# Loading the query weights ahead of the third modulation chunk, and projecting the queries in two contraction halves

## The chip, the cores and the metric

The kernel runs on one core of one Trainium2 chip. The metric is device time in microseconds (us), the median of repeated executions. The core has a tensor engine for matrix products (PE; its weight loads are listed as PEld), a vector engine (DVE), a scalar engine (ACT), GpSimd (POOL), and a sync engine (SP) whose in-order instruction stream issues nearly all of the large transfers.

## The reference, cut to what matters

Two transformer blocks are computed on 256 tokens of width 1024, in float32. Only the opening of the first block bears on the change:

```
sh1, sc1, gt1, sh2, sc2, gt2 = modulation(c, w_mod, b_mod)      # silu(c) @ w_mod + b_mod, 6 x 1024 columns
hx = rms_norm(x, norm1_g) * (1 + sc1) + sh1                     # 256 tokens
hc = rms_norm(ctx, norm1_g) * (1 + csc1) + csh1                 # 256 context rows, same w_mod with c_ctx
q, k, v, gb, gc, u = split(hx @ w_in)                           # 512 | 128 | 128 | 512 | 512 | 512 columns
q, k = rms_norm per head of 64, then rotary for the tokens of x
```

From the context only k and v are used. Then come attention, a short convolution of `gc * u` gated by `gb`, the output projection, a mixture of 32 experts (each with three weight matrices of 3 MB), and a second block with retention, stick-breaking attention and a SwiGLU layer.

## The kernel before

**Layout.** `hT` holds the normalized inputs turned, as 8 contraction blocks (c = 0 to 7) of 128 rows by 512 columns: columns 0 to 255 are the context (row tiles t = 0, 1), 256 to 511 the tokens (t = 2, 3). `PS` is the accumulator memory, 8 banks of 512 columns. Shift and scale enter `hT` in two halves. Half 0 (blocks 0 to 3) needs the modulation chunks W_A 0 and 1, half 1 (blocks 4 to 7) the chunks W_A 2 and 3. When a half's modulation is turned (`turned_A`), the vector engine forms the scales (lines 1107 to 1115) and modulates the context columns (line 1119), and the scalar engine the token columns (line 723).

**The ring of weights.** The list `order` (line 297) gives the order in which SP issues the weight chunks of this opening, and the slot of each. All are 2 MB except the key and value weights W_KV (1 MB). Before an issue, SP waits until the chunk that held the same slot has been used (line 492): W_GB goes into the slot of W_A 2, W_B 2 into that of W_A 3, W_GC into that of W_B 0, W_U into that of W_B 1, W_B 3 into that of W_Q. W_Q has the wait of line 500 besides, on the second normalized tile.

**The tensor engine's order** (lines 2012 to 2040). `keys_values(0)` multiplies the first four blocks for all four row tiles into banks 4 to 7 and leaves the sums open. `modulate_A(2)`, `modulate_A(3)` and `turned_A(1)` follow, with `keep_busy` matmuls of no use to the result between them. `keys_values(1)` closes the sums. `project` computes the queries of t = 2 and then of t = 3, 8 blocks each. `conv_blocks(W_GB, 0)` follows, then the transposes of the finished queries and keys (line 2030, behind `qk_ready` 4), then `conv_blocks(W_GC, CV)`, the first attention scores, and the rest of the modulation (`modulate_B`).

**The vector engine's order** (lines 1134 to 1170). In this order it treats the keys of t = 0 and t = 1 (norm only), `accumulated(0)` and `accumulated(1)`, the queries and keys of t = 2 (sums of squares, gains, norm and rotary, lines 1143 to 1166), `accumulated(2)`, the queries and keys of t = 3, and `accumulated(3)`. An `accumulated(k)` multiplies the 128 by 4096 chunk W_B k by a column of the condition and adds it to the sum so far, so that the tensor engine can do the first four of the eight W_B chunks in one pass (lines 1127 and 1130). The end of `accumulated(1)` frees the slot for W_GC, that of `accumulated(2)` the slot for W_U. The scalar engine copies the projections out of `PS` and squares them (lines 737 to 745), and GpSimd forms the reciprocal roots (lines 622 to 624).

Of the kernel before, what the change touches and what calls it, by code (L numbers as in the profile page):

```python
# [10 lines left out]
ACT = mybir.ActivationFunctionType  # L11
AX = mybir.AxisListType.X

P = 128
D = 1024
KD = D // P
# [53 lines left out]
def build(nc, A, out):  # L70

    ctx = ExitStack()
    with ctx:
# [4 lines left out]
        PS = ctx.enter_context(nc.psum_tensor("PS", [P, 8, 512], F32))  # L78
# [20 lines left out]
        def shaped(ap, *dims):  # L99
            if len(dims) == 2:  # L100
                return ap.rearrange("p (a b) -> p a b", a=dims[0])
            if len(dims) == 3:
                return ap.rearrange("p (a b c) -> p a b c", a=dims[0], b=dims[1])
            return ap

        def flat(ap):
            return ap.rearrange("p a b -> p (a b)")
# [70 lines left out]
        hT = slot4.take(KD, 512)  # L178
# [91 lines left out]
        S = {}  # L270
        for n in ("ld_consts ld_x ld_ctx ld_c ld_vec ld_rows cleared set_cond cond_ready "
# [22 lines left out]

        W_A, W_B, W_KV, W_Q, W_GB, W_GC, W_U = range(7)
        ACC = 3
        order = [(W_A, 0, 0), (W_A, 1, 1), (W_KV, 0, 4), (W_A, 2, 2), (W_A, 3, 3), (W_Q, 0, 5), (W_B, 0, 0), (W_B, 1, 1),
                 (W_GB, 0, 2), (W_B, 2, 3), (W_GC, 0, 0), (W_U, 0, 1), (W_B, 3, 5), (W_B, 4, 3), (W_B, 5, 2), (W_B, 6, 0), (W_B, 7, 5)]
        columns = {W_KV: (512, 256), W_Q: (0, 512), W_GB: (768, 512), W_GC: (1280, 512), W_U: (1792, 512)}
        freed = {W_Q: ("qkv_psum", 6), W_GB: ("gbgc_psum", 4), W_GC: ("gbgc_psum", 8), W_U: ("u_psum", 4)}  # L300
# [14 lines left out]
        def chunk(kind, i=0):  # L315
            if kind == W_KV:
                return w_kv
            home = ring[slot_of[kind, i]]
            if kind == W_A:
                return shaped(home, KD, CW)  # L320
            return home if kind == W_B else shaped(home, KD, CW)

        def chunk_landed(eng, kind, i=0):
            eng.wait_ge(w_full[slot_of[kind, i]], landed[kind, i])
# [97 lines left out]
        def chunk2(name, i):  # L422
            n = C2[name, i]
            dims = seconds[n][1]
            size = 1
            for d in dims:
                size *= d
            return shaped(cslots[:, n % CSLOTS, 0:size], *dims)
# [54 lines left out]
        def _(sp):  # L483
# [100 lines left out]
            for n, (src, dims, _, _) in enumerate(seconds):  # L584
                if n >= CSLOTS:
                    sp.wait_ge(S[seconds[n - CSLOTS][2]], seconds[n - CSLOTS][3])
                size = 1
                for d in dims:
                    size *= d
                dst = shaped(cslots[:, n % CSLOTS, 0:size], *dims)  # L590
                parts = [(dst[:, :, u], src[:, :, u]) for u in range(2)] if len(dims) == 3 else [(dst, src)]
                for to, of in parts:
                    sp.dma_start(to, of).then_inc(c_full[n % CSLOTS], 16)
# [85 lines left out]
        def _(a):  # L679
# [47 lines left out]
            def head_sumsq(t):  # L727

                if t >= 1:
                    a.wait_ge(S["qksq_sum"], t)  # L730
                a.drain()
                o = 512 if t < 2 else 0
                a.activation(qk_sq[:, o:640], qk[:, t, o:640], ACT.Square).then_inc(S["qksq_done"], 1)
# [7 lines left out]
            for t in range(2, 4):  # L741
                a.wait_ge(S["qkv_psum"], t + 3)
                a.activation(qk[:, t, 0:512].rearrange("p (j g d) -> p g j d", g=2, j=4),
                             PS[:, t, :].rearrange("p (g j d) -> p g j d", g=2, j=4), ACT.Copy).then_inc(S["qkv_evac"], 1)
                head_sumsq(t)

            for m in range(8):
# [1137 lines left out]
        def _(pe):  # L1885
            mm = pe.matmul
# [7 lines left out]
            def keep_busy(bank, n):  # L1894

                for _ in range(n):
                    mm(PS[:, bank, 0:P], ident, ident, start=True, stop=True, skip_group_check=True)
# [15 lines left out]
            def modulate_A(k):  # L1913

                half, u, w = k // 2, k % 2, chunk(W_A, k)
                chunk_landed(pe, W_A, k)
                for c in range(KD):
                    for gg in range(4):
                        last = mm(PS[32 * gg:32 * gg + 32, 1 - half, P * u:P * u + P], condT[:, c, :], w[:, c, P * gg:P * gg + P],
                                  start=c == 0, stop=c == KD - 1, skip_group_check=True)  # L1920
                last.then_inc(S["mod_psum"], 1)

            def turned_A(half):

                pe.wait_ge(S["modA_evac"], half + 1)
                transposes(2 + half, [modA[:, P * n:P * n + P] for n in (2 * half, 2 * half + 1)]).then_inc(S["modT_psum"], 1)
# [35 lines left out]
            for c in range(KD):  # L1962
                last = pe.transpose(PS[:, 3, META * c:META * c + META], metahn[:, P * c:P * c + P], ident[0:META, 0:META])
# [1 line left out]
            turned_A(0)  # L1965


            def project(bank, kind, t):

                w = chunk(kind)  # L1970
                width = columns[kind][1]
                for c in range(KD):
                    last = mm(PS[:, bank, 0:width], hT[:, c, P * t:P * t + P], w[:, c, :], start=c == 0, stop=c == KD - 1)
                last.then_inc(S["qkv_psum"], 1)

            def keys_values(half):

                w = chunk(W_KV)
                for t in range(4):
                    for c in range(4 * half, 4 * half + 4):  # L1980
                        if t in (0, 2):
                            pe.wait_ge(S["hTc_ready" if t == 0 else "hTx_ready"], c + 1)
                        last = mm(PS[:, 4 + t, 0:256], hT[:, c, P * t:P * t + P], w[:, c, :], start=c == 0, stop=c == KD - 1,
                                  skip_group_check=True)
                    if half:
                        last.then_inc(S["qkv_psum"], 1)
# [26 lines left out]
            chunk_landed(pe, W_KV)  # L2013
            pe.wait_ge(S["xnT_evac"], 8)
            keys_values(0)
            modulate_A(2)
            keep_busy(1, 2)
            modulate_A(3)
            keep_busy(1, 1)
            turned_A(1)  # L2020
            keep_busy(1, 4)
            keys_values(1)
            chunk_landed(pe, W_Q)
            for t in range(2, 4):
                project(t, W_Q, t)
            pe.wait_ge(S["qkv_evac"], 4)
            conv_blocks(W_GB, 0)
            pe.wait_ge(S["qk_ready"], 4)
# [13 lines left out]
            for b in range(2):  # L2042
                last = mm(PS[:, 6 + b, :], K["headmean"], flat(sqT)[:, 512 * b:512 * b + 512], start=True, stop=True)
# [83 lines left out]
            for i in range(KD // 2):  # L2127
                for k in range(2):
                    mm(PS[64 * k:64 * k + 64, 6, TOK:TOK + 1], w_route[:, 2 * i + k, :], shT[:, 2 * i + k:2 * i + k + 1],
                       start=i == 0, stop=i == KD // 2 - 1, skip_group_check=True)  # L2130
# [9 lines left out]
            for t in range(TT + 1):  # L2140
                rows = lgT[:, P * t:P * t + P] if t < TT else lgT[:, TOK:TOK + 1].to_broadcast([P, P])
                last = mm(PS[:, 7, NR * t:NR * t + EG + E], rows, K["fold"], start=True, stop=True, skip_group_check=True)
# [95 lines left out]
            for n in range(4):  # L2238
                t, h = n // 2, n % 2
# [5 lines left out]
            def block_T(bank, w, col, rhs, n, off=0, start=True, halves=False):  # L2245

                for c in range(KD):
                    if halves and c == KD // 2:
                        pe.wait_ge(S["hnT_ready"], 2)
                    last = mm(PS[:, bank, off:off + n], w[:, c, col:col + P], rhs(c), start=c == 0, stop=c == KD - 1,  # L2250
                              skip_group_check=True)
                return last
# [160 lines left out]
            for n in range(2 * RH):  # L2413
                name, h = ("rq" if n < RH else "rk"), n % RH
                chunk2_landed(pe, name, h // 2)
                w = chunk2(name, h // 2)
# [7 lines left out]
                for i in range(2):  # L2424
                    last = block_T(2 * (n % 2) + i, w, 256 * (h % 2) + P * i, x_of if n < RH else all_of,
                                   TOK if n < RH else LK)
# [4 lines left out]
            for h in range(RH):  # L2431
# [3 lines left out]
                for keys, q0, off in ((META, 0, 0), (META + P, P, TOK)):  # L2435
                    for d in range(2):
                        mm(PS[:, 4 + h % 2, off:off + TOK - q0], kR[:, 2 * h + d, keys:keys + P], qR[:, 2 * h + d, q0:TOK],
                           start=d == 0, stop=d == 1, skip_group_check=True)
                for d in range(2):
                    for gg in range(4):  # L2440
                        last = mm(PS[32 * gg:32 * gg + 32, 6 + h % 2, 0:TOK], kR[:, 2 * h + d, 0:32], qR[:, 2 * h + d, :],
                                  start=d == 0, stop=d == 1, skip_group_check=True)
# [32 lines left out]
            for h in range(RH):  # L2475
# [6 lines left out]
                for cc in range(2):  # L2482
                    for gg in range(4):
                        last = mm(PS[32 * gg:32 * gg + 32, 3, :], hnT[:, 2 * gg + cc, 0:32], rv[:, 2 * gg + cc, :],  # L2484
                                  start=cc == 0, stop=cc == 1, skip_group_check=True)
# [104 lines left out]
            w = chunk2("fi", 0)  # L2590
            for t in range(TT):
                pe.wait_ge(S["hnT_ready"], 3 + t)
                for u in range(2):
                    for i in range(2):
                        for c in range(KD):
                            o = TOK * i + P * t
                            last = mm(PS[:, u, o:o + P], w[:, c, u, P * i:P * i + P], hnT[:, c, P * t:P * t + P],  # L2597
                                      start=c == 0, stop=c == KD - 1, skip_group_check=True)
# [60 lines left out]
            def out_product(j, k):  # L2659

                bank, x, w = out_products(j)[k]
                return mm(PS[:, bank, :], x, w, start=j == 0, stop=j == FB // 2 - 1, skip_group_check=True)  # L2662

            for j in range(2 * FO_MAIN):
                if j % 2 == 0:
                    pe.wait_ge(S["combined"], fo_combined("w", j // 2))
                for k in range(7):
# [6 lines left out]
                    last = out_product(j, k)  # L2674
# [4 lines left out]
            for k in range(7):  # L2679
                for j in range(2 * FO_MAIN, FB // 2):  # L2680
                    if k == 0 and j % 2 == 0:
                        pe.wait_ge(S["combined"], fo_combined("w", j // 2))
                    last = out_product(j, k)
# [70 lines left out]
```

## Time and profile before

| what | value |
|---|---|
| median of 3 runs | 1547.5 us (1546.63 to 1547.79) |
| the profiled execution | 1550.47 us |
| its span in the trace | 1548.7 us |
| mean granted clock of the tensor engine | 0.936 of 2.4 GHz |
| PE, DVE, ACT, POOL busy | 83%, 35%, 13%, 2% of the span |

The profiled execution is 1.8 us longer than its span and 3.0 us longer than the median. The opening up to the first attention scores takes the first 96 us of the span. The experts run from 196 us to about 861 us and move most of the bytes.

### The profile page before, as it was taken

How to read it: one execution, taken by the hardware profiler on the slowest of the kernel's cores; microseconds unless marked ns; L12 is line 12 of the kernel's file. 1: busy time of each engine (PE TensorE's matmuls, PEld its weight loads, DVE VectorE, ACT ScalarE, POOL GpSimd, SP SyncE). 2: the span in 40 equal slices, each digit the busy share in tenths (PEclk: the TensorE clock that was granted, in tenths of full speed). 3: DMA queues.
4: the chain of work that ended last, by engine and by line, in shares of the span. 5: the costliest groups of instructions: out<-in, count | busy, mean ns of one | idle time of the engine just before them, and what ended most of it. 6: DMA issues, size and time to landing. Idle time of an engine off the chain costs nothing.

```text
span 1548.7 us, 25300 instructions
## 1 busy us (share of the span) xinstructions
PE 1284.8 (83%) x11090; PEld 834.0 (54%) x11090; DVE 542.5 (35%) x977; ACT 204.1 (13%) x429; POOL 33.8 (2%) x66
## 2 busy tenths in 40 slices
PE   6999977666666666666665999999999999999998
PEld 5786555344333333333433766458544477688843
DVE  1556432111111111111111312752446463466654
ACT  4214200000000000000000223320011211211101
POOL 1101000000000000000000100000000000000000
PEclk9999999888888888888877999999999999999999
DMA  9879999999999999999999733333244344445551
GB/s 348 317 304 324 381 390 428 431 430 432 430 431 431 430 433 428 431 431 430 432 428 422 265 120 109 140 132 140 103 156 145 109 155 171 134 145 174 173 190 54
DMA packets 86431, 447.43 MB, mean 289 GB/s; under 512 B 4012, under 2 KB 27728, under 8 KB 72672
## 3 DMA queue, kind: packets, MB, share of 16 engines
q1 hardware_dynamic: 84096, 441.20, 71.1%
q10 hardware_dynamic: 1008, 3.77, 0.6%
q0 software_dynamic: 1264, 1.55, 0.4%
q8 instruction: 48, 0.79, 0.2%
q14 instruction: 15, 0.12, 0.0%
HBM read 445.44 MB, written 1.06 MB: 288 GB/s over the span
## 4 chain that ended last, share of the span: by engine, by line
PE 55%; DMA 33%; issue 5%; DVE 3%; DVEq 1%; ACT 1%; POOL 1%; POOLq 0%; ACTq 0%
DMA mem<-in_w_down 33%; PE PS L2613 8%; PE PS L2250 8%; PE PS L2268 7%; PE PS L2456 6%; PE PS L2206 5%; PE PS L2662 4%; PE PS L2189 2%; PE PS L2075 2%; PE PS L1999 2%; PE PS L1891 2%; PE PS L1901 2%; PE PS L2567 1%; PE PS L2597 1%; PE PS L2484 0%
## 5 line engine op out<-in xcount | busy, mean ns | idle before, releaser
L2189 PE MATMUL PS<-mem 128*32 128x192 f32 x4096 | 207.2, 362 | 106.3 <-DMA mem<-in_w_up 72.4
L2189 PEld LDWEIGHTS PS<-mem 128*32 128x32 f32 x4096 | 150.4, 122 | 157.1 <-DMA mem<-in_w_up 82.1
L2206 PE MATMUL PS<-mem 128*32 128x256 f32 x1536 | 137.3, 530 | 99.4 <-DMA mem<-in_w_down 91.9
L2206 PEld LDWEIGHTS PS<-mem 128*32 128x32 f32 x1536 | 62.3, 148 | 167.4 <-DMA mem<-in_w_down 98.0
L2268 PE MATMUL PS<-mem 128*128 128x256 f32 (+1 forms) x392 | 125.1, 474 | 2.6 <-issue 1.1
L2613 PE MATMUL PS<-mem 128*128 128x256 f32 x560 | 122.6, 379 | 0.0
L2250 PE MATMUL PS<-mem 128*128 128x256 f32 (+1 forms) x512 | 117.2, 390 | 0.0
L1365 DVE TENSOR_TENSOR mem<-mem,PS 128x192 f32<-128x192 f32 x32 | 11.3, 354 | 298.7 <-ACT mem L803 298.7
L2613 PEld LDWEIGHTS PS<-mem 128*128 128x128 f32 x560 | 105.6, 190 | 14.2 <-ACT mem L1037 0.3
L2250 PEld LDWEIGHTS PS<-mem 128*128 128x128 f32 x512 | 97.4, 192 | 18.6 <-issue 1.8
L2456 PE MATMUL PS<-mem 128*128 128x512 f32 x224 | 98.4, 594 | 0.7 <-ACT mem L938 0.7
L2268 PEld LDWEIGHTS PS<-mem 128*128 128x128 f32 x392 | 72.9, 190 | 46.4 <-issue 38.8
L1369 DVE TENSOR_TENSOR mem<-PS,mem 128x256 f32<-128x256 f32 x32 | 13.6, 425 | 196.4 <-PE PS L2206 196.4
L2456 PEld LDWEIGHTS PS<-mem 128*128 128x128 f32 x224 | 41.9, 190 | 53.3 <-issue 51.8
L2662 PE MATMUL PS<-mem 128*128 128x512 f32 x154 | 66.4, 592 | 0.0
L801 ACT ACTIVATE mem<-PS 128x256 f32<-128x256 f32 x32 | 12.3, 384 | 338.3 <-PE PS L2167 338.3
L2213 PE MATMUL PS<-mem 32*128 32x256 f32 x512 | 36.7, 400 | 17.6 <-DVE mem L1369 17.6
L803 ACT ACTIVATE mem<-PS 128x192 f32<-128x192 f32 x32 | 10.6, 331 | 302.8 <-PE PS L2189 302.8
L1901 PEld LDWEIGHTS PS<-mem 128*128 128x128 f32 x296 | 35.4, 145 | 26.6 <-issue 11.6
L1901 PE MATMUL PS<-mem 128*128 128x128 f32 x296 | 42.8, 283 | 7.2 <-DVE mem L1445 2.4
L2662 PEld LDWEIGHTS PS<-mem 128*128 128x128 f32 x154 | 29.2, 190 | 35.9 <-issue 35.9
L2213 PEld LDWEIGHTS PS<-mem 32*128 32x128 f32 x512 | 23.1, 184 | 37.1 <-DVE mem L1369 36.4
(340 smaller groups left out, 1341.2 us busy)
## 6 DMA issues: line engine op xcount, KB each, us to landing
mem<-in_w_gate SPq DMA_DIRECT2D x31, 3072.0 KB, 38.7
mem<-in_w_down SPq DMA_DIRECT2D x31, 3072.0 KB, 38.7
mem<-in_w_up SPq DMA_DIRECT2D x30, 3072.0 KB, 39.4
mem<-in_w_in SPq DMA_DIRECT2D x26, 2048.0 KB, 7.8
mem<-in_w_mod SPq DMA_DIRECT2D x12, 2048.0 KB, 17.6
mem<-in_w_ffn_in SPq DMA_DIRECT2D x22, 1024.0 KB, 6.7
mem<-in_w_ffn_out SPq DMA_DIRECT2D x5, 2048.0 KB, 7.9
mem<-in_w_ret_out SPq DMA_DIRECT2D x4, 2048.0 KB, 7.9
```

Source lines behind the costliest of these rows:

```text
L1891: last = mm(PS[0:m, bank, 0:n], lhs(c), w[:, c, col0:col0 + n], start=c == 0, stop=c == KD - 1)
L1901: last = pe.transpose(PS[:, bank, rows * i:rows * i + rows], s, ident[0:rows, 0:rows])
L1999: last = mm(PS[:, 6 + m % 2, 0:TOK], w[:, c, P * (m % 4):P * (m % 4) + P], hT[:, c, TOK:2 * TOK], start=c == 0, stop=c == KD - 1)
L2075: last = mm(PS[:, 2 + n, :], mixT[:, first + c, P * t:P * t + P], weights[:, c, CW * o:CW * o + CW], start=start and c == 0, stop=stop and ...
L2189: last = mm(PS[32 * gg:32 * gg + 32, 2 * h + 1, 192 * j:192 * j + 192], xTe[:, h, c, :], rows[:, 192 * gg:192 * gg + 192], start=c == 0 an ...
L2206: last = mm(PS[32 * gg:32 * gg + 32, 2 * h, 0:256], hTe[:, h, j, :], slots[:, 3 * h + 2, o:o + 256], start=j == 0, stop=j == JE - 1, skip_ ...
L2213: last = mm(PS[:, 4 + gg, 256 * t:256 * t + 256], back[own, h, P * t:P * t + P], yexp[own, h, :], start=False, stop=True, skip_group_check ...
L2250: last = mm(PS[:, bank, off:off + n], w[:, c, col:col + P], rhs(c), start=c == 0, stop=c == KD - 1, skip_group_check=True)
L2268: last = mm(PS[:, bank, 0:width], x[:, c, :], w[:, c, :], start=product in ("m1", "m2", "m7") and c == 0, stop=product in ("m2", "m4", "m3 ...
L2456: last = mm(PS[:, bank, :], x[:, c, :], w[:, c, :], start=start and c == 0, stop=stop and c == 3, skip_group_check=True)
L2613: last = mm(PS[:, fi_bank(bank, j), 0:256], x[:, c, :], part[:, c, :], start=start and c == 0, stop=stop and c == 3, skip_group_check=True)
L2662: return mm(PS[:, bank, :], x, w, start=j == 0, stop=j == FB // 2 - 1, skip_group_check=True)
```

## The change

The query weights are issued before W_A 2 and 3 and not behind them. `project`, which ran behind `keys_values(1)`, gives way to `queries(half)`: `queries(0)` multiplies blocks 0 to 3 for t = 2 and t = 3 straight after `keys_values(0)` and leaves both sums open, and `queries(1)` closes them behind `keys_values(1)`. The queries accumulate in banks 1 and 2, and no longer in 2 and 3, since `turned_A(1)` writes bank 3 in between. The `keep_busy` matmuls around `modulate_A(3)` are left out, and the last ones go to bank 0.

```
-        order = [(W_A, 0, 0), (W_A, 1, 1), (W_KV, 0, 4), (W_A, 2, 2), (W_A, 3, 3), (W_Q, 0, 5), (W_B, 0, 0), (W_B, 1, 1),
+        order = [(W_A, 0, 0), (W_A, 1, 1), (W_KV, 0, 4), (W_Q, 0, 5), (W_A, 2, 2), (W_A, 3, 3), (W_B, 0, 0), (W_B, 1, 1),
@@ scalar engine, evacuation of the queries
-                             PS[:, t, :].rearrange("p (g j d) -> p g j d", g=2, j=4), ACT.Copy).then_inc(S["qkv_evac"], 1)
+                             PS[:, t - 1, :].rearrange("p (g j d) -> p g j d", g=2, j=4), ACT.Copy).then_inc(S["qkv_evac"], 1)
@@ tensor engine
-            def project(bank, kind, t):
-
-                w = chunk(kind)
-                width = columns[kind][1]
-                for c in range(KD):
-                    last = mm(PS[:, bank, 0:width], hT[:, c, P * t:P * t + P], w[:, c, :], start=c == 0, stop=c == KD - 1)
-                last.then_inc(S["qkv_psum"], 1)
+            def queries(half):
+
+                w = chunk(W_Q)
+                for t in (2, 3):
+                    for c in range(4 * half, 4 * half + 4):
+                        last = mm(PS[:, t - 1, :], hT[:, c, P * t:P * t + P], w[:, c, :], start=c == 0, stop=c == KD - 1,
+                                  skip_group_check=True)
+                    if half:
+                        last.then_inc(S["qkv_psum"], 1)
@@
             keys_values(0)
+            chunk_landed(pe, W_Q)
+            queries(0)
             modulate_A(2)
-            keep_busy(1, 2)
             modulate_A(3)
-            keep_busy(1, 1)
             turned_A(1)
-            keep_busy(1, 4)
+            keep_busy(0, 4)
             keys_values(1)
-            chunk_landed(pe, W_Q)
-            for t in range(2, 4):
-                project(t, W_Q, t)
+            queries(1)
             pe.wait_ge(S["qkv_evac"], 4)
             conv_blocks(W_GB, 0)
```

## Rows read from the trace of the kernel before

**Rows 1.** The page: span, and the chain that ended last, by line.
```profile
span 1548.7 us, 25300 instructions
DMA mem<-in_w_down 33%; PE PS L2613 8%; PE PS L2250 8%; PE PS L2268 7%; PE PS L2456 6%; PE PS L2206 5%; PE PS L2662 4%; PE PS L2189 2%; PE PS L2075 2%; PE PS L1999 2%; PE PS L1891 2%; PE PS L1901 2%; PE PS L2567 1%; PE PS L2597 1%; PE PS L2484 0%
```

**Rows 2.** Chain of waits, 0 to 190 us: start, duration, what.
```profile
80.46 0.33 DVE mem L1165
...
81.07 1.53 PE PS L1901 x12
82.61 13.81 PE PS L1999 x64
```

**Rows 3.** Timeline of PE: start, duration, line, operation, count, idle before and releaser.
```profile
31.13 7.14 PE L1983 MATMUL PS<-mem 128*128 128x256 f32 x32 [0.51 <-DVE mem L1119]
38.20 1.95 PE L1919 MATMUL PS<-mem 128*32 128x128 f32 x64
...
40.73 1.95 PE L1919 MATMUL PS<-mem 128*32 128x128 f32 x64
...
43.19 0.44 PE L1901 MATMUL PS<-mem 128*128 128x128 f32 x2
...
44.93 7.17 PE L1983 MATMUL PS<-mem 128*128 128x256 f32 x32 [0.41 <-DVE mem L1119]
51.94 13.90 PE L1973 MATMUL PS<-mem 128*128 128x512 f32 x32
65.68 13.98 PE L1999 MATMUL PS<-mem 128*128 128x256 f32 x64
81.07 1.53 PE L1901 MATMUL PS<-mem 128*128 128x128 f32 x12 [1.42 <-DVE mem L1166]
```

**Rows 4.** Timeline of DVE, 52 to 92 us.
```profile
52.28 2.35 DVE L1127 TENSOR_SCALAR mem<-mem 128x4096 f32<-128x4096 f32 x1
...
60.46 0.82 DVE L1143 TENSOR_REDUCE mem<-mem 128x10 f32<-128x640 f32 x1 [1.27 <-ACT mem L733]
...
68.63 4.48 DVE L1130 SCALAR_TENSOR_TENSOR mem<-mem 128x4096 f32<-128x4096 f32 x1 [0.16 <-issue]
73.03 0.81 DVE L1143 TENSOR_REDUCE mem<-mem 128x10 f32<-128x640 f32 x1
...
80.70 0.32 DVE L1166 TENSOR_TENSOR mem<-mem 128x160 f32<-128x160 f32 x1
87.05 4.49 DVE L1130 SCALAR_TENSOR_TENSOR mem<-mem 128x4096 f32<-128x4096 f32 x1 [6.03 <-DMA mem<-in_w_mod]
```

**Rows 5.** SP's issues of W_A 2, W_Q and W_GB, each with its time to landing.
```profile
L495 SPq DMA_DIRECT2D mem<-in_w_mod x1: 5204/5204/5204, 14.6 to 14.6; - x1
...
DMA to landing us min/median/max: 18.9/18.9/18.9
...
L502 SPq DMA_DIRECT2D mem<-in_w_in x1: 4489/4489/4489, 25.1 to 25.1; - x1
...
DMA to landing us min/median/max: 19.2/19.2/19.2
...
L502 SPq DMA_DIRECT2D mem<-in_w_in x1: 378/378/378, 40.2 to 40.2; - x1
...
DMA to landing us min/median/max: 19.4/19.4/19.4
```

**Rows 6.** Timeline of PE: first matmuls after idle stretches of 1.4 to 4.5 us.
```profile
25.16 3.60 PE L1919 MATMUL PS<-mem 128*32 128x128 f32 x64 [2.04 <-DMA mem<-in_w_mod]
...
244.70 2.80 PE L2206 MATMUL PS<-mem 128*32 128x256 f32 x48 [1.42 <-DVE mem L1367]
...
303.45 5.26 PE L2206 MATMUL PS<-mem 128*32 128x256 f32 x48 [4.50 <-DMA mem<-in_w_down]
```

**Rows 7.** Stages: window, length, busy PE, PEld, DVE, ACT, POOL, granted clock, DMA share, GB/s.
```profile
26.00:27.00 1.00, 1.00 (x28) 0.92 (x21) 0.00 (x0) 0.00 (x0) 0.00 (x0) 0.50 1.04 378
304.00:306.00 2.00, 2.00 (x24) 0.87 (x20) 0.00 (x0) 0.00 (x0) 0.00 (x0) 0.50 0.97 418
```

## The prediction

> **What bounds the kernel now.** I read the page first. Its chain that ended last runs for a third of the span through the expert weights, then through the matmuls of the second block; of the opening only small shares show [rows 1]. The opening feeds what follows without slack: the first expert weights are issued behind semaphores that the tensor engine raises late in the opening (mod_psum 9 and later ones), so a shift of the opening's end shifts the start of the expert stream by as much. What the change is worth must therefore be read from the first 100 us.
>
> There I read the chain of waits. At 81 us it steps from the vector engine's last rotary instruction (line 1166) to the tensor engine's transposes of queries and keys, and stays on the tensor engine from there, first with the 13.8 us of the W_GC block [rows 2]. The tensor engine's timeline says how close that is. It is busy almost without a gap from 31 us, ends the W_GB block at 65.68 + 13.98 = 79.66, and sits idle 1.42 us until line 1166 is done [rows 3]. So two chains end at 81 us: the tensor engine's, with 1.4 us to spare, and the vector engine's, which ends last.
>
> The vector engine's timeline shows what the second is made of: `accumulated(0)` at 52.28, then `accumulated(1)`, then t = 2 from 60.46 to 68.5, `accumulated(2)` from 68.63, t = 3 from 73.03 to 81.02 [rows 4]. In all this it waits for the projections only once, 1.27 us ahead of 60.46, for the square of the queries of t = 2 [rows 4]; waits of about 2 us on GpSimd's roots lie inside each of the two treatments and stay there. So the chain hangs on the time at which it starts, and that is the time at which `keys_values(1)` runs (44.93), since the keys of t = 0 and t = 1 stand first in the vector engine's order.
>
> **The change part by part.** Everything is worked out in the profiled execution.
>
> *Order of the transfers.* The fourth issue (W_A 2 before) landed at 14.6 + 18.9 = 33.5, the sixth (W_Q before) at 25.1 + 19.2 = 44.3 [rows 5]. All of these are 2 MB, so I let the places keep their times: W_Q lands at 33.5, W_A 2 at about 39.0 (the fifth place, in the middle), W_A 3 at 44.3. The wait on the second normalized tile, which now stands in front of two W_A issues on SP, costs nothing: the tile is the second result of the whole vector engine, and SP comes to the wait only behind its issue of W_KV, at 14.6 [rows 5].
>
> *queries(0).* It starts when `keys_values(0)` ends, at 31.13 + 7.14 = 38.2, and W_Q has landed 4.7 us earlier. It is half of the 16 products that took 13.90 us [rows 3], 6.95 us, and ends at 45.15.
>
> *modulate_A(2), (3), turned_A(1).* W_A 2 (39.0) is there. Without the filler between them the two modulations take 1.95 us at most each, where 2.53 us passed from start to start before (38.20 to 40.73) [rows 3]: 0.6 us saved. `modulate_A(3)` wants W_A 3 at about 47.1 and that lands at 44.3, so it waits for nothing, with 2.8 us to spare. The filler left out behind it lay within the wait for the scalar engine's copy and saves nothing. From the start of `modulate_A(3)` to that of `keys_values(1)` it is 44.93 - 40.73 = 4.2 us, a path through the scalar and the vector engine with four filler matmuls over it, unchanged.
>
> So `keys_values(1)` starts 6.95 - 0.6 = 6.35, say 6.3 us later, at 51.2, and with it everything that follows from the second half of the modulation.
>
> *queries(1).* `keys_values(1)` ends at 58.4, and 6.95 us later, at 65.3, the queries are complete (65.8 before). For the tensor engine the change is a gain of 0.5 to 0.6 us. t = 2 is complete at 58.4 + 3.5 = 61.9, and 1.6 us behind that (51.94 + 6.95 = 58.9 to 60.46 before) its squares can be summed: 63.5.
>
> *The vector engine.* `accumulated(0)` starts at 52.28 + 6.3 = 58.6. It and `accumulated(1)` took until 60.46 - 1.27 = 59.2; now until 65.5. The squares of t = 2 have been there since 63.5, so the wait of 1.27 us goes, and nothing else does. t = 2 runs from 65.5, and from there all is as before, 5.0 us later (6.3 - 1.27): `accumulated(2)` at 73.7 (W_B 2, needed at 68.6 before, comes no later than then), t = 3 until 81.0 + 5.0 = 86.1. The tensor engine has ended the W_GB block at 65.3 + 13.98 = 79.3 and waits 6.8 us for it. **The transposes start 5.0 us late.**
>
> *Slots and queues behind it.* W_GB waits for `modulate_A(2)`, now done at 47.1 where its issue was at 40.2. It landed at 40.2 + 19.4 = 59.6, after so long because it stood behind others in the queue [rows 5], which are still there at 47.1. I expect it at about 59.6 again; at worst it takes the full 19.4 us anew and lands at 66.5, 1.2 us after it is wanted, which the 6.8 us of idle time would hide. W_GC is issued at the end of `accumulated(1)`, 6.3 us late, and wanted at 87.6; even if it took the 19.4 us of W_GB it would be there at 84.9. W_U and W_B 3 go with `accumulated(2)`, 5.0 us late, and with them `accumulated(3)`, which waited for W_B 3 until 87.05 [rows 4]. All of this is the same shift of 5.0 and adds nothing.
>
> *The clock.* Not covered by any of this is what 6.8 us of idle time do to the tensor engine. After 2.04 us idle the 64 matmuls of one `modulate_A` took 3.60 us [rows 6] where they take 1.95 [rows 3], and the granted clock was 0.50, the 1.2 GHz level [rows 7]: a loss of 1.65 us. After 4.50 us idle 48 matmuls took 5.26 us where the same took 2.80 after 1.42 us idle [rows 6], a loss of 2.46, again at 0.50 [rows 7]. The stretch of 6.8 us is longer than both. I bound the cost by 0 and 2.5 us and take 1.7, near the first: there the tensor engine had a long unbroken run of work behind the gap, as here. The loss falls on the transposes and on the W_GC block, which stand on the chain [rows 2], and is not made up.
>
> The Trainium skill (TensorE: Matmul & The Clock Gate, "What's actually happening") says of the ramp that for modeling it is under 1% of a typical span and that one should not fit to a count of slow matmuls. By that the term would be left out and the kernel would come to 1552.5. This case's trace shows 1.65 and 2.46 us for single ramps, small against the span, though a third of the effect here.
>
> **The sum.** 5.0 + 1.7 = 6.7 us on the profiled execution of 1550.5. The same shift on the median of 1547.5, which is 3.0 us below it, gives 1554.2.
>
> **The rivals.**
>
> *The clock holds, or its loss is hidden* (12%): 5.0 us alone, 1552.5. For it: the idle time of 1.42 us at 81 us cost nothing. Against it: each of the longer gaps above did.
>
> *The tensor engine sets the end* (8%), the rival on the other side, not slower. Then the 0.6 us of filler counts and the vector engine doesn't: 1546.9, no measurable change. It holds if the vector engine ends t = 3 before 79.3, so if its chain is 7 us shorter than I have it. That wants the two large accumulations (2.35 and about 4.5 us) to be out of the way before the second half of the keys comes. For it speaks that W_B 0 and 1 are issued early, right behind W_A 3. Against it: they stand behind the keys of t = 1 in program order, and the vector engine takes its instructions in order.
>
> *The weights come late* (8%): if W_Q in front pushes W_A 3 back by a further transfer (5.3 us, the distance of two places), `modulate_A(3)` waits 5.3 - 2.8 = 2.5 us, and the vector engine's chain with it: 1556.7. For it: nothing but that places may not keep their times. Against it: the same bytes in the same queue, in which each waits 19 us for its landing [rows 5].
>
> *The shift is absorbed later* (5%), in the expert stage, where transfers limit: 1547.5 to 1549. Against it: these transfers are issued by the opening's own events, so the stream itself starts late.
>
> **How the numbers follow.** The forecast, 1554.2, has 67%; its own range is 1553 to 1555.5, from the clock term. For 8 times in 10 I add the clock-free case below and late weights above: 1551.8 to 1556.8. What a measurement of this kernel can tell from no change is about 0.2%, 3.1 us. Slower by more: the forecast, the clock-free case (5.0) and late weights, 87%. Within it: the tensor engine's rival and absorption, 11%. Faster: 2%.
>
> **What would show it.** In the changed kernel's trace: the second half of keys and values at 51.2 us and not 44.9; the reduction of t = 2 starting without a wait at 65.5; W_GB's block ending at 79.3; the tensor engine idle 6 to 7 us and released by line 1166 at 86.1; a granted clock of 0.50 in the 1 to 4 us behind that; the first scores 6 to 7 us later than 96.4, where the W_GC block ended [rows 2]. Wrong I would be if the vector engine's accumulations stood ahead of the wait, if the tensor engine waited in `modulate_A(3)`, or if the first expert's products did not come 6 to 7 us later.

## The result, and the profile after

| | before | changed |
|---|---|---|
| median | 1547.07 us (4 runs, 1546.18 to 1547.79) | 1558.87 us (4 runs, 1557.66 to 1559.15) |
| profiled execution, its span | 1550.47, 1548.7 | 1557.66, 1555.9 |

The changed kernel is slower by 11.8 us, a ratio of 1.0078 (95% interval 1.0065 to 1.0091). The forecast was 6.7 us, and the time lies above the range. The direction and, in the main, the mechanism in the opening were right. Some 5.6 us came from a place that the prediction never looked at, 750 us later.

**The opening.** The timeline of the tensor engine in the changed kernel answers to [rows 3] (L1985 is `keys_values`, L1973 the queries, L2001 `conv_blocks`):

```profile
27.05 7.14 PE L1985 MATMUL PS<-mem 128*128 128x256 f32 x32 [0.50 <-DVE mem L1119]
34.03 7.03 PE L1973 MATMUL PS<-mem 128*128 128x512 f32 x16
40.99 1.95 PE L1919 MATMUL PS<-mem 128*32 128x128 f32 x64
43.42 1.95 PE L1919 MATMUL PS<-mem 128*32 128x128 f32 x64 [0.47 <-DMA mem<-in_w_mod]
...
47.62 7.17 PE L1985 MATMUL PS<-mem 128*128 128x256 f32 x32 [0.41 <-DVE mem L1119]
54.63 7.03 PE L1973 MATMUL PS<-mem 128*128 128x512 f32 x16
61.49 13.98 PE L2001 MATMUL PS<-mem 128*128 128x256 f32 x64
82.38 2.82 PE L1901 MATMUL PS<-mem 128*128 128x128 f32 x12 [6.91 <-DVE mem L1166]
85.00 14.74 PE L2001 MATMUL PS<-mem 128*128 128x256 f32 x64
```

The wait of 6.91 us for line 1166 stands where it was forecast (6.8), released by the engine that was forecast. One sign of being wrong is there too: `modulate_A(3)` (the second L1919 line) waited for a transfer, if only 0.47 us. The vector engine's timeline, which answers to [rows 4], shows its chain without the wait of 1.27 us ahead of t = 2:

```profile
57.38 4.48 DVE L1130 SCALAR_TENSOR_TENSOR mem<-mem 128x4096 f32<-128x4096 f32 x1
61.79 0.81 DVE L1143 TENSOR_REDUCE mem<-mem 128x10 f32<-128x640 f32 x1
...
69.94 4.48 DVE L1130 SCALAR_TENSOR_TENSOR mem<-mem 128x4096 f32<-128x4096 f32 x1 [0.16 <-issue]
74.35 0.81 DVE L1143 TENSOR_REDUCE mem<-mem 128x10 f32<-128x640 f32 x1
```

In the stages around the wait (columns as in [rows 7]) the granted clock falls to the 1.2 GHz level while the tensor engine is idle, and is there still when it resumes:

```profile
79.00:82.00 3.00, 0.00 (x0) 0.00 (x0) 2.78 (x11) 0.00 (x0) 3.00 (x6) 0.62 1.12 435
82.00:85.00 3.00, 2.62 (x13) 2.62 (x13) 0.33 (x2) 0.00 (x0) 0.42 (x1) 0.50 1.02 424
87.00:89.00 2.00, 2.00 (x11) 1.74 (x11) 0.77 (x1) 0.00 (x0) 0.00 (x0) 1.00 0.33 21
```

The transposes took 2.82 us for 1.53 and the W_GC block 14.74 for 13.98 [rows 3], 2.05 us together.

**An execution that was late at the start.** In the profile of before, `keys_values(0)` starts at 31.13 [rows 3], in the changed kernel at 27.05, although nothing ahead of it was changed. Before had waited 2.04 us for W_A 1 and then run it at half the clock [rows 6]; here W_A 1 came by 22.74. That is chance. Of the eight profiles in the old order of transfers (before and seven experiments), two show such a wait of 2 us, before and experiment 12, and only that of before shows the fall of the clock; experiment 8, in the new order, shows both again. The profiled execution of before lay 3.4 us above the median of the table, and this late start accounts for most of it: its transposes stood at 81.07, and those of the seven experiments in the old order at 78.1 to 79.0. The profiled execution of the changed kernel lay 1.2 us below its own median. So the two profiles put the changed kernel only 7.2 us behind, where the medians say 11.8.

**The last expert.** L2162 stands for the first matmuls of an expert, L2213 for its last. At 26 of the first 31 L2213 groups the changed kernel is 3.0 to 3.4 us behind the late profile of before. In the 32nd and last expert it falls back by 5.6 more. The tensor engine's timeline of before:

```profile
835.47 1.15 PE L2213 MATMUL PS<-mem 32*128 32x256 f32 x16 [0.54 <-DVE mem L1369]
843.19 1.93 PE L2162 MATMUL PS<-mem 128*32 128x256 f32 x16 [6.57 <-issue]
...
859.66 1.15 PE L2213 MATMUL PS<-mem 32*128 32x256 f32 x16 [0.55 <-DVE mem L1369]
```

and of the changed kernel:

```profile
838.40 1.15 PE L2213 MATMUL PS<-mem 32*128 32x256 f32 x16 [0.54 <-DVE mem L1369]
846.27 1.07 PE L2162 MATMUL PS<-mem 128*32 128x256 f32 x5 [6.73 <-issue]
852.08 1.92 PE L2162 MATMUL PS<-mem 128*32 128x256 f32 x11 [4.73 <-issue]
...
868.16 1.15 PE L2213 MATMUL PS<-mem 32*128 32x256 f32 x16 [0.55 <-DVE mem L1369]
```

From one L2213 to the next it is 24.19 us before and 29.76 after. Both have a stop ahead of the last expert's first matmul for which the profile names no releaser ("issue"), and the changed kernel has a second, after 5 matmuls of one group of 16. The page's list of DMA queues has one with the name "instruction", first before, then changed:

```profile
q8 instruction: 48, 0.79, 0.2%
```
```profile
q8 instruction: 49, 0.80, 0.2%
```

The packets are of 16 KB (0.79 MB / 48). Their number is no sign of a second stop: experiments 3, 4 and 5 have 49 packets and only one such stop. Their times are what counts. In the changed kernel one packet lies at 843.5 us and one at 849.5, each ahead of the end of a stop, while all queues together move 400 GB/s. In the profile of before they lie at 840.25 and 846.25, as far apart, but the second holds nothing up: the 16 matmuls from 843.19 on run through. All fourteen profiles have the second packet about 6 us behind the first. So the question is how soon the engine needs what the second brings. In the code, the last expert stands in each arm of a branch on the number of extra sweeps (lines 2227 and 2235). The arm taken lies behind the other, which holds hundreds of instructions, so it is reached by a jump. And the changed kernel has 12 instructions fewer on the tensor engine ahead of it (25288 in its profile, 25300 before), the three fillers left out: a float32 filler shows as two weight loads and two matmuls.

The Trainium skill (Runtime: NRT & Kernel Launch, "Instruction fetch mechanics") says that instructions come in blocks of 16 KiB, 256 instructions, one after the other, and that a taken branch to a block that is not at hand forces a fetch that execution waits for. The packets' size and the stop behind the jump agree; the experiments below test the rest.

### The profile page after: what moved, and what is told of

It is laid out like the page before. It is cut to its first block, busy times and chain, and to the rows that moved or that the text cites. A ratio compares the mean times of both kernels' runs of the same rounds, so it can differ in the third digit from the quotient of the medians.

```text
span 1555.9 us, 25288 instructions
## 1 busy us (share of the span) xinstructions
PE 1281.3 (82%) x11084; PEld 833.8 (54%) x11084; DVE 542.2 (35%) x977; ACT 204.0 (13%) x429; POOL 33.6 (2%) x66
## 4 chain that ended last, share of the span: by engine, by line
PE 54%; DMA 34%; issue 6%; DVE 3%; DVEq 1%; POOL 1%; ACT 1%; POOLq 0%; ACTq 0%
DMA mem<-in_w_down 34%; PE PS L2613 8%; PE PS L2250 7%; PE PS L2268 7%; PE PS L2456 6%; PE PS L2206 5%; PE PS L2662 4%; PE PS L2001 2%; PE PS L2075 2%; PE PS L1891 2%; PE PS L1901 2%; PE PS L2189 1%; PE PS L2567 1%; PE PS L2597 1%; PE PS L2484 0%
## 5 line engine op out<-in xcount | busy, mean ns | idle before, releaser
L2189 PE MATMUL PS<-mem 128*32 128x192 f32 x4096 | 202.9, 356 | 104.1 <-DMA mem<-in_w_up 71.8
L2206 PE MATMUL PS<-mem 128*32 128x256 f32 x1536 | 139.5, 536 | 103.1 <-DMA mem<-in_w_down 97.0
L2613 PEld LDWEIGHTS PS<-mem 128*128 128x128 f32 x560 | 105.6, 190 | 14.2 <-ACT mem L1037 0.3
L1901 PE MATMUL PS<-mem 128*128 128x128 f32 x296 | 43.4, 286 | 13.1 <-DVE mem L1166 6.9
L1901 PEld LDWEIGHTS PS<-mem 128*128 128x128 f32 x296 | 36.1, 147 | 32.6 <-issue 11.6
L2213 PE MATMUL PS<-mem 32*128 32x256 f32 x512 | 36.7, 400 | 17.6 <-DVE mem L1369 17.6
L2162 PE MATMUL PS<-mem 128*32 128x256 f32 x512 | 36.2, 393 | 11.9 <-issue 11.5
```

The source lines that it names most:

```text
L1901: last = pe.transpose(PS[:, bank, rows * i:rows * i + rows], s, ident[0:rows, 0:rows])
L2162: last = mm(PS[32 * gg:32 * gg + 32, 2 * h, 0:256], pick[:, h, t, :], xrow[:, t, 256 * gg:256 * gg + 256], start=t == 0, stop=t == TT - 1, ...
L2189: last = mm(PS[32 * gg:32 * gg + 32, 2 * h + 1, 192 * j:192 * j + 192], xTe[:, h, c, :], rows[:, 192 * gg:192 * gg + 192], start=c == 0 an ...
L2206: last = mm(PS[32 * gg:32 * gg + 32, 2 * h, 0:256], hTe[:, h, j, :], slots[:, 3 * h + 2, o:o + 256], start=j == 0, stop=j == JE - 1, skip_ ...
L2213: last = mm(PS[:, 4 + gg, 256 * t:256 * t + 256], back[own, h, P * t:P * t + P], yexp[own, h, :], start=False, stop=True, skip_group_check ...
L2613: last = mm(PS[:, fi_bank(bank, j), 0:256], x[:, c, :], part[:, c, :], start=start and c == 0, stop=stop and c == 3, skip_group_check=True)
```

## The experiments

Runs of a group share a chip and their runs of the kernel before (medians 1546.30, 1546.23 and 1546.25 us). Theory A was the place of the code: the engine fetches its instructions in 16 KB pieces, and with 12 instructions fewer the jump lands just ahead of a piece's end, so that the next piece is soon waited for too. Theory B was the phase of the expert stage against its transfers.

**1. The three fillers left out of the kernel before.**

```
             modulate_A(2)
-            keep_busy(1, 2)
             modulate_A(3)
-            keep_busy(1, 1)
```

> The kernel before, with nothing but the three filler matmuls around modulate_A(3) left out (12 instructions fewer on the tensor engine, as in the changed kernel). The changed kernel came out 11.8 us slower where I had 6.7. Its trace has the predicted idle time and clock loss in the opening, and besides them a second stop of 4.7 us in the last expert, after 5 matmuls of line 2162, beside a 16 KB instruction transfer. Theory A (place of the code): the last expert is reached by a jump over the code of the branch above it, its instructions are fetched in 16 KB pieces, and with 12 instructions fewer ahead of it the jump lands shortly before the end of a piece, so that a second fetch is waited for: this kernel has the second stop too and is 4 to 5 us slower than before (+4.6: 5.2 less 0.6 saved in the opening). Theory B (phase): the stop comes from the shift of the expert stage against the weight transfers: no second stop here, and 0 to 1 us faster than before.

Measured 1552.37 us, 1.0036 (1.0022 to 1.0050), 6.1 us slower. The second stop is there, after the same 5 matmuls (the lines shift by the edit, L2160 is L2162 above):

```profile
841.07 1.07 PE L2160 MATMUL PS<-mem 128*32 128x256 f32 x5 [5.92 <-issue]
847.04 1.92 PE L2160 MATMUL PS<-mem 128*32 128x256 f32 x11 [4.91 <-issue]
```

The opening gained nothing, where I had 0.6 us: `modulate_A(3)` now waited 1.93 us for W_A 3, which lands at 38.0 (1.33 us in experiment 4, with the fillers). The fillers had stood in that wait. So half of the changed kernel's loss can be had from the kernel before by taking out work that does nothing.

**2. The changed kernel with 12 instructions put back, in its idle time.**

```
+            keep_busy(3, 3)
             pe.wait_ge(S["qk_ready"], 4)
```

> The changed kernel with three filler matmuls (12 instructions) put back, but in the idle time ahead of the transposes of the queries, where they cost nothing. Theory A (place of the code): the second stop in the last expert goes, and the kernel is about 5 us faster than the changed one, 6.5 to 7 us slower than before, which is the forecast of the prediction. Theory B (phase of the expert stage): nothing changes, 11 to 12 us slower than before.

Measured 1552.18 us, 1.0035 (1.0024 to 1.0046), 5.9 us slower than before. The last expert has one stop again:

```profile
844.05 1.94 PE L2163 MATMUL PS<-mem 128*32 128x256 f32 x16 [6.71 <-issue]
```

What is left is the opening. This is the plainest comparison of the study: the change as it is, with as many instructions ahead of the jump as before.

**3. The changed kernel with wide fillers in its idle time.**

```
+            for _ in range(6):
+                mm(PS[:, 3, :], ident, consts[:, 0:512], start=True, stop=True, skip_group_check=True)
             pe.wait_ge(S["qk_ready"], 4)
```

> The changed kernel with six wide filler matmuls (512 columns, about 0.87 us each, 5.2 us in all, 24 instructions) in the idle time of 6.9 us ahead of the transposes. The clock's share by itself: if the idle time makes the tensor engine fall to 1.2 GHz, the granted clock stays at 1.00 here and the transposes and the W_GC block take 15.5 us and not 17.6; against the kernel with three narrow fillers this one is 2 us faster, 4.5 to 5 us slower than before. If the clock costs nothing on the path, the two are equal. The instructions are 12 more than before, which by theory A keeps the jump's landing clear of the end of a piece.

Measured 1551.09 us, 1.0028 (1.0016 to 1.0040), 4.8 us slower than before. The granted clock, in the stage that had 0.50 above, and the matmuls behind the wait:

```profile
82.00:85.00 3.00, 2.66 (x18) 2.51 (x19) 0.28 (x2) 0.00 (x0) 0.39 (x1) 1.00 1.00 418
```
```profile
82.34 1.53 PE L1901 MATMUL PS<-mem 128*128 128x128 f32 x12 [1.78 <-DVE mem L1166]
83.70 13.98 PE L2001 MATMUL PS<-mem 128*128 128x256 f32 x64
```

In the trace the W_GC block ends 2.3 us earlier than in experiment 2 (97.7 against 100.0), but at the 31st expert's L2213 its profile is 1.9 us behind that of experiment 2 (838.07 against 836.19), and the medians differ by 1.1 us with overlapping intervals. The clock's loss is shown in the opening; what it costs in device time is not resolved.

**4. The last expert ahead of the branch.** On the kernel before:

```
             expert(PAIRS - 1, 0, (PAIRS - 1) * 4 + 1)
+            expert(PAIRS - 1, 1, (PAIRS - 1) * 4 + 3, last_one=True)
             pe.wait_ge(S["route_ready"], 1)
...
             with pe.If(extra > 0):
-                expert(PAIRS - 1, 1, (PAIRS - 1) * 4 + 3, last_one=True)
...
             with pe.If(extra < 1):
-                expert(PAIRS - 1, 1, (PAIRS - 1) * 4 + 3, last_one=True)
                 keep_busy(0, 16)
```

> The kernel before, with the 32nd expert's instructions on the tensor engine issued ahead of the branch on the number of extra sweeps and not once in each of its arms; the work is the same. By theory A the first stop of 6.6 us ahead of the last expert comes from the jump over the untaken arm, so it goes here, and the last expert is then bound by its weights: 4 to 6 us faster than before. By theory B the stop is a wait that goes with the end of the loop or with the transfers, and the time is that of before.

Measured 1546.54 us, 1.0003 (0.9993 to 1.0012): no gain, where I had expected 4 to 6 us. The stop moved with the jump:

```profile
832.19 1.15 PE L2213 MATMUL PS<-mem 32*128 32x256 f32 x16 [0.54 <-DVE mem L1369]
833.26 1.07 PE L2162 MATMUL PS<-mem 128*32 128x256 f32 x16
...
852.80 1.15 PE L2213 MATMUL PS<-mem 32*128 32x256 f32 x16 [0.55 <-DVE mem L1369]
860.21 5.96 PE L1897 MATMUL PS<-mem 128*128 128x128 f32 x32 [6.26 <-issue]
866.00 1.91 PE L1901 MATMUL PS<-mem 128*128 128x128 f32 x16
```

The last expert has no stop and takes 20.6 us instead of 24.2, but now the fillers behind the branch wait 6.26 us, and being late and at half the clock they hold up the transposes of the second block.

**5. As 4, with the 16 fillers ahead of the branch too.**

```
             expert(PAIRS - 1, 1, (PAIRS - 1) * 4 + 3, last_one=True)
+            keep_busy(0, 16)
             pe.wait_ge(S["route_ready"], 1)
...
-            with pe.If(extra < 1):
-                keep_busy(0, 16)
```

> The kernel before with the 32nd expert ahead of the branch on the number of extra sweeps, and the 16 filler matmuls that follow it ahead of the branch too. In the run with the expert alone moved, the stop went from in front of the expert (6.6 us) to in front of these fillers (6.26 us), and the transposes behind them (line 1901) came at 866.0, where they could have started at about 860 by the vector engine. If the stop is the fetch of the jump's target, it now comes behind the fillers (3.84 us at full clock), partly under the 7.3 us that the vector and scalar engines take anyway: the transposes at about 862 to 864, 1.5 to 3 us faster than before. If the stop has another cause (the value load or the branch itself) it is as long but independent of the transfers in flight.

Measured 1545.29 us, 0.9990 (0.9980 to 1.0000), the edge of what can be told from no change, where I had expected 1.5 to 3 us. The transposes came at 863.14, within the 862 to 864 of the expectation, behind a stop of 4.96 us.

**6. As 5, without the 16 fillers.** The line added in 5 is left out.

> As the run with the fillers first, but without these 16 fillers: the jump is taken at 854 us, its fetch ends by 860.3, and the transposes start as soon as the vector engine has its rows (about 860.3). Fetch theory: 2 to 4 us faster than before, less a clock loss of 1.5 to 2.5 us in the matmuls behind 8 us of idle time, so 0 to 2.5 us faster. If the idle time didn't lower the clock, 3.5 us faster.

Measured 1543.14 us, 0.9987 (0.9977 to 0.9997): the fastest kernel of the study, 3.1 us by the medians and 2.0 by the ratio. The transposes are released by the vector engine, and no stop is left:

```profile
859.75 3.36 PE L1901 MATMUL PS<-mem 128*128 128x128 f32 x16 [6.15 <-DVE mem L1445]
```

The packets of the jump's target and of the next piece are there, at 857.0 and 863.0; the first lies within the wait for the vector engine, the second at the end of the 16 transposes.

**7. The third accumulation behind the queries of t = 3**, in experiment 2's kernel:

```
-                if t == 3:
-                    accumulated(2)
...
+            accumulated(2)
             accumulated(ACC)
```

> The changed kernel with three fillers in the idle time, and with the third accumulation of the modulation weights (4.48 us) on the vector engine behind the queries of t = 3, not ahead of them. It tells whether the vector engine's order makes the idle time of 6.9 us: if so the transposes start 4.5 us earlier, at 77.7 and not 82.1, and the tensor engine waits 1.5 to 2 us for them, without the fall of the clock. If something else releases them (the weights, the slots), they stay at 82. What comes behind isn't meant to be good: the loads of W_U and W_B 3 are issued 4.5 us later and with them the last accumulation, so that the scores wait and the time as a whole is no better than 1552.

A single run, 1556.8 us. The tensor engine's timeline:

```profile
77.42 1.53 PE L1900 MATMUL PS<-mem 128*128 128x128 f32 x12 [1.78 <-DVE mem L1164]
78.78 13.98 PE L2000 MATMUL PS<-mem 128*128 128x256 f32 x64
101.16 3.79 PE L2009 MATMUL PS<-mem 64*128 64x512 f32 x8 [8.39 <-DVE mem L1174]
```

The transposes are 4.7 us earlier and at full clock (forecast 4.5): the vector engine's order makes the idle time. The gain is given back at once. W_B 3 is issued later, the last accumulation waits 12.82 us for it, and the scores wait 8.39 us for the copies behind that.

**8. The order of the transfers alone**, on the kernel before: the first line of the diff and nothing else.

> The kernel before with the query weights issued ahead of W_A 2 and 3, and nothing else changed: the same instructions on the tensor engine. In the other runs W_A 3 landed at 38.0 in the old order and at 43.4 in the new, and modulate_A(3) waited for it in both. So the order by itself puts the second half of keys and values at 47.6 and not 42.3: the vector engine's chain starts 5.3 us later, as in the changed kernel. But the queries of t = 2 come later too (61.6), and the W_GB block ends at 82.5: the transposes at about 83.9 after 1.4 us of idle time, no loss of clock, no second stop in the last expert. Expected 5 to 6 us slower than before. If the order is free, as the prediction had it (2.8 us to spare), the time is that of before.

Measured 1551.27 us, 1.0026 (1.0015 to 1.0038), 5.0 us slower.

```profile
43.56 1.95 PE L1919 MATMUL PS<-mem 128*32 128x128 f32 x64 [2.81 <-DMA mem<-in_w_mod]
...
47.76 7.17 PE L1983 MATMUL PS<-mem 128*128 128x256 f32 x32 [0.41 <-DVE mem L1119]
54.77 13.90 PE L1973 MATMUL PS<-mem 128*128 128x512 f32 x32
68.50 13.98 PE L1999 MATMUL PS<-mem 128*128 128x256 f32 x64
83.89 1.53 PE L1901 MATMUL PS<-mem 128*128 128x128 f32 x12 [1.41 <-DVE mem L1166]
```

The transposes are where they were expected. `keys_values(1)` starts at 47.76, as late as in the changed kernel (47.62), with no query matmul ahead of it. The late W_A 3 alone makes the whole shift. The queries in halves (experiment 2, 5.9 us) gain nothing over this; whether they lose the 0.9 us between the two medians can't be told.

**9. The edits of experiment 6 on the changed kernel.**

> The changed kernel with the edits of the fastest run so far (32nd expert ahead of the branch, its 16 fillers left out). It takes the jump out of the changed kernel's last expert. If the 11.8 us are the opening's 6.0 and the last expert's 5.2, the second stop can't fall there any more and what is left against the same edits of the kernel before (1543.1) is the opening alone: about 1549.1, 3 us slower than before. Were the place of the code not the cause, it would be some 11 us above 1543.1, at 1554 to 1555.

Measured 1555.22 us, 1.0065 (1.0048 to 1.0082), 12.1 us above experiment 6, where 6 were expected. The trace says why:

```profile
864.42 1.33 PE L1901 MATMUL PS<-mem 128*128 128x128 f32 x5 [6.16 <-DVE mem L1445]
870.19 2.51 PE L1901 MATMUL PS<-mem 128*128 128x128 f32 x11 [4.45 <-issue]
```

The last expert is clean, and the second stop is back behind the jump's new landing, again after 5 matmuls. The time by itself, 1555.2, is near the 1554 to 1555 that the expectation gave for the case that the place of the code is not the cause; only the trace tells the two apart. Between the profiled executions of experiments 6 and 9 it is 10.3 us (spans of 1541.3 and 1551.6), of which 5.1 are there at the scores and 4.45 are the stop. What I had taken for safe was a new draw.

**10. Experiment 6 with the three fillers of the opening left out.**

> The fastest run so far with the three fillers around modulate_A(3) left out as well, 12 instructions fewer. With the jump ahead of the last expert gone, these 12 instructions cost nothing there: 1543.1 again, give or take 1, if the new landing of the jump lies clear of the end of a piece. If it is 4 to 6 us slower, the lottery of the place has moved to the new landing (a second stop in the transposes or the first products of the second block).

Measured 1548.74 us, 1.0013 (1.0004 to 1.0023), above experiment 6 by 5.6 us by the medians and 4.0 by the ratios. The alternative in the expectation is what happened:

```profile
859.49 1.33 PE L1901 MATMUL PS<-mem 128*128 128x128 f32 x5 [6.17 <-DVE mem L1445]
865.55 2.50 PE L1901 MATMUL PS<-mem 128*128 128x128 f32 x11 [4.73 <-issue]
```

**11 and 12. Two fillers out, one filler out**, on the kernel before: `keep_busy(1, 2)` alone, and `keep_busy(1, 1)` alone.

> The kernel before without the two fillers between modulate_A(2) and (3): 8 instructions fewer. In the runs with 12 fewer, the second stop in the last expert came after 5 matmuls of line 2162 (10 instructions with their weight loads). If it marks the end of a 16 KB piece, then with 4 instructions more ahead of the jump's landing it comes after 3 matmuls. If it had to do with time or transfers, it would be at another place or gone. About 5 us slower than before.

> The kernel before without the one filler behind modulate_A(3): 4 instructions fewer. By the same count the second stop comes after 1 matmul of line 2162. The filler lies in a wait of the opening, so the opening is unchanged, and the whole is about 5 us slower than before for four instructions of no use less.

A single run each, 1553.48 and 1551.63 us. First 11, then 12:

```profile
841.21 1.05 PE L2161 MATMUL PS<-mem 128*32 128x256 f32 x3 [6.12 <-issue]
846.78 1.93 PE L2161 MATMUL PS<-mem 128*32 128x256 f32 x13 [4.51 <-issue]
```
```profile
839.37 0.62 PE L2161 MATMUL PS<-mem 128*32 128x256 f32 x1 [6.26 <-issue]
844.76 1.93 PE L2161 MATMUL PS<-mem 128*32 128x256 f32 x15 [4.78 <-issue]
```

Three matmuls and one, as counted: 4 instructions are two matmuls with their weight loads. The stop sits at a fixed place among the instructions and moves by the instructions removed ahead of it. Theory B has no way to say that. With the packets ahead of the stops' ends, this leaves theory A.

## Why the prediction was wrong, step by step

**The failed step: what was left out of the account.** The prediction priced the removed fillers by their time alone, 0.6 us saved. That they are also 12 instructions, and that 750 us further on a jump lands so that with 12 fewer in front of it the next piece of code is waited for too, was in no term of the sum and in no rival. It is worth 5.6 us in the trace (24.19 us before and 29.76 after for the last expert), 6.1 by experiment 1, and 5.9 by experiment 2 (11.8 less 5.9). The first stop was in the trace of before, 6.57 us with no releaser, and I had not asked what it was.

**Order of the transfers: wrong, but without effect on the sum.** I gave W_A 3 2.8 us to spare, and the fillers 0.6 us. Both came from the late profiled execution. In the usual one the tensor engine is 4 us earlier while the transfers behind W_A 1 keep their times. W_A 3 was waited for before the change (until 38.0 to 38.7 in six of the seven experiments in the old order) and as a rule after it (43.2 to 43.6; in experiments 2 and 7 the tensor engine came just as it had landed). Experiment 4 stands for the old order:

```profile
38.08 1.95 PE L1919 MATMUL PS<-mem 128*32 128x128 f32 x64 [1.33 <-DMA mem<-in_w_mod]
...
42.27 7.17 PE L1983 MATMUL PS<-mem 128*128 128x256 f32 x32 [0.41 <-DVE mem L1119]
```

The places in the queue did keep their times, as the prediction had it: the sixth lands at 43.4, where I had 44.3. What was wrong is when the tensor engine comes. The shift of `keys_values(1)` is one 2 MB transfer, 5.35 us against experiment 4 (42.27 to 47.62), and not 6.95 less 0.6. Experiment 8 shows it alone. Since both limits are nearly equal (the wait left over is 0.47 us), 6.3 and 5.35 are close; that is luck.

**queries(0), queries(1): right.** 7 us each, and the W_GB block followed the second without a wait for its weights (issued at 43.0 and landed at 58.6, wanted at 61.5), so that the tensor engine was 6.9 us early for the transposes.

**The vector engine's chain: right.** The wait of 1.27 us went, nothing else. In the usual execution of the old order the vector engine stands idle elsewhere: `accumulated(1)` waits 1.3 to 1.5 us for W_B 1, and t = 2 follows without a wait, 15.5 us behind the start of `keys_values(1)` as in the late one. In the changed kernel it is 14.2. So the transposes came 4.0 us later than in experiment 4 (78.40 to 82.38), where I had 5.0; the difference is that `keys_values(1)` shifted by 5.35 and not 6.3.

**The slots behind it: right.** No weight of the later blocks was waited for longer than before; the last accumulation waited 5.91 us for W_B 3, as 6.03 before [rows 4].

**The clock: right, a little small.** 2.05 us where I took 1.7, within the bounds of 0 and 2.5. By the same two lines it is 1.9 us in experiment 9 and 2.6 in experiment 2, just above the bound.

**The sum.** The opening cost 6.0 us (the scores at 99.66 against 93.67 in experiment 4; 93.3 to 94.2 in 1, 10, 11 and 12) where I had 6.7. With 5.6 in the last expert that makes 11.6 of the 11.8 measured. The sum is put together from several executions, and the close fit is in part luck: from the scores to the 31st expert's L2213 it is 736.2 to 741.0 us in the fourteen profiles, and 1.3 of the 8.5 us between the two profiles at the transposes of the second block (866.95 and 875.46) are gone by the end, which I did not follow. The shift went through the expert stage as forecast (against experiment 4 it is 6.0 us at the scores and 6.2 at the 31st expert's L2213); the rivals "tensor engine sets the end" and "absorbed" are refuted. "The weights come late" was half right: `modulate_A(3)` did wait, 0.47 us where the rival had 2.5, but since the tensor engine was early and not since W_A 3 was late.

## What to carry to other kernels

An edit of an engine's instruction stream also moves all code behind it. Look in the trace for stops without a releaser behind jumps, and keep the count of instructions ahead of a jump equal in a comparison before believing a difference of a few microseconds. Where a stop is hidden, as in experiment 6, it can be back with the next edit.

Ask of a profiled execution that lies above the median where it was late, before taking slack from it: a wait hidden by one late transfer is a wait in the others.

A transfer moved forward moves others back by its own length. If the one moved back feeds two engines and the slower of them has no slack, the work that fills the wait is no gain.

## What the runs showed of the hardware

The stop at the jump's target was 5.9 to 6.7 us in ten profiles and 4.96 in experiment 5, while the transfers ran at about 400 GB/s; in experiments 6, 9 and 10 it lies under a wait of 6.2 us for the vector engine. The stop for the next piece, where there was one, was 4.4 to 4.9 us more. The second packet is there with and without such a stop, about 6 us behind the first, so the second stop is about what the matmuls ahead of the piece's end leave of these 6 us. That the full DMA queues make the fetch so long is not shown: no run has the jump with idle queues. Elsewhere in the kernel before, with its 48 packets, no idle stretch without a releaser is longer than 1.1 us.

The execution-to-execution chance in the landing of the second transfer (22.7 to 25.2 us) moves the tensor engine by up to 4 us at 27 us and by 2.1 to 3.0 at the transposes in the old order; in the new order hardly anything is left of it at `keys_values(1)` (47.1 to 47.6 and, in the late execution of experiment 8, 47.76), since W_A 3 lands at 43.2 to 43.6 in either case and sets that start, or comes just in time for it.
